# Last two expert blocks formed from PSUM in two extra output tiles of a one-core hybrid decoder step

## The reference, cut to what matters

```python
def hier_moe(h, ...):                       # 1056 tokens: 1024 prompt rows and 32 sample rows
    ...                                     # group, then two experts of 32 per token, with gates
    order = jnp.argsort(e_flat)             # the 2112 assignments sorted by expert
    padded = (counts + MOE_BLOCK - 1) // MOE_BLOCK * MOE_BLOCK
    ...
    def expert_block(args):                 # 128 rows of one expert
        e, tok = args
        xb = x_pad[tok]
        hmid = jax.nn.silu(xb @ w_gate[e]) * (xb @ w_up[e])
        return hmid @ w_down[e]
    out = lax.map(expert_block, ...) * buf_w[:, None]
    y = jax.ops.segment_sum(out, buf_tok, num_segments=n_tok + 1)[:n_tok]
...
h = x + mix                                 # decoder_layer
h = h + hier_moe(rms_norm(h, norm_ffn_w), ...)
y_prompt, y_sample = rms_norm(yp, norm_final_w), rms_norm(ys, norm_final_w)
```

## Time and profile before

| what | value |
|---|---|
| time, median of 3 runs (lowest to highest) | 1505.89 us (1504.56 to 1506.14) |
| time of the profiled execution | 1505.11 us |
| its span in the trace | 1503.4 us |
| busy PE / DVE / ACT / POOL | 1416.1 / 1061.5 / 766.1 / 568.4 us |
| HBM read / written | 316.52 MB / 59.64 MB |

### The profile page before, as it was taken

The page is one execution under the profiler, slowest core; times in us unless marked ns, Lnnn a source line. Parts: engine busy times, 40 slices in busy tenths (PEclk is TensorE's granted clock), DMA queues, the critical chain, the costliest instruction groups (busy, mean ns, idle before and its releaser), DMA issues. The chain is left out here.

```text
span 1503.4 us, 21686 instructions
## 1 busy us (share of the span) xinstructions
PE 1416.1 (94%) x7625; PEld 1233.0 (82%) x7625; DVE 1061.5 (71%) x1225; ACT 766.1 (51%) x891; POOL 568.4 (38%) x345
## 2 busy tenths in 40 slices
PE   6999999999999999899999659999999999999976
PEld 5999999999999998788877548888888888888852
DVE  6687722366666664545463579999999999999956
ACT  6332222333333335344433438777777777777734
POOL 2323324454444442485644014333433333333311
PEclk9999999999999999999999669999999999999997
DMA  5222333234444445876653659999999999999958
GB/s 197 65 78 86 126 95 111 80 130 143 144 141 147 138 144 167 294 219 239 209 168 130 231 201 383 402 396 390 377 381 362 389 379 383 385 388 387 369 211 343
DMA packets 115793, 361.07 MB, mean 240 GB/s; under 512 B 18772, under 2 KB 48468, under 8 KB 99348
## 3 DMA queue, kind: packets, MB, share of 16 engines
q1 hardware_dynamic: 100164, 322.37, 58.6%
q0 software_dynamic: 15568, 37.87, 7.3%
HBM read 316.52 MB, written 59.64 MB: 250 GB/s over the span
## 5 line engine op out<-in xcount | busy, mean ns | idle before, releaser
L2048 DVE TENSOR_TENSOR wgu_l<-wgu,wgu_h 128x2048 fp32r<-128x2048 f32 x128 | 290.0, 2288 | 27.4 <-ACT wgu_h L1928 26.5
L1928 ACT CAST wgu_h<-wgu 128x2048 fp32r<-128x2048 f32 x124 | 237.4, 1915 | 100.6 <-PE bank0and L64 100.5
L62 PE MATMUL bank0and<-wgu_h,xh_blk 128*128 128x512 f32 x512 | 203.7, 398 | 2.9 <-DVE xl_blk L2052 2.9
L64 PE MATMUL bank0and<-wgu_h,xl_blk 128*128 128x512 f32 x512 | 200.9, 392 | 0.0
L62 PE MATMUL bank0and<-xh,wh 128*128 128x352 f32 x576 | 197.6, 343 | 3.0 <-ACT raw L906 3.0
L63 PE MATMUL bank0and<-wgu_l,xh_blk 128*128 128x512 f32 x512 | 200.3, 391 | 0.0
L64 PE MATMUL bank0and<-xh,wl 128*128 128x352 f32 x576 | 186.7, 324 | 0.0
L63 PE MATMUL bank0and<-xl,wh 128*128 128x352 f32 x576 | 186.5, 324 | 0.0
L1671 POOL TENSOR_TENSOR wol<-wo,woh 128x1024 fp32r<-128x1024 f32 x48 | 121.4, 2536 | 123.5 <-ACT woh L996 123.5
L1835 POOL DMA_INDIRECT scratch_picked<-yb,dst x31 | 92.7, 2991 | 197.5 <-DVE yb L2042 197.5
L2057 DVE TENSOR_TENSOR wd_l<-wd,wd_h 128x1024 fp32r<-128x1024 f32 x128 | 148.2, 1219 | 1.2 <-ACT wd_h L1934 1.0
(11 more groups left out here) (496 smaller groups left out, 3234.5 us busy)
## 6 DMA issues: line engine op xcount, KB each, us to landing
wgu<-in_w_gate_up SPq DMA_DIRECT2D x128, 1024.0 KB, 7.6
wd<-in_w_down SPq DMA_DIRECT2D x128, 512.0 KB, 7.6
wo<-in_w_out SPq DMA_DIRECT2D x48, 512.0 KB, 4.9
w<-in_w_in_tiles SPq DMA_DIRECT2D x36, 512.0 KB, 3.6
yy<-scratch_picked SPq DMA_DIRECT2D x8, 1024.0 KB, 12.6
scratch_xb<-stage POOLq DMA_DIRECT2D x10, 512.0 KB, 4.0
xb<-scratch_xb SPq DMA_DIRECT2D x8, 640.0 KB, 4.4
scratch_uT<-feat SPq DMA_DIRECT2D x8, 528.0 KB, 5.0
```

The lines of the kernel that those rows point to most:

```text
L62: nc.tensor.matmul(acc, lh, rh, start=start, stop=False)
L64: return nc.tensor.matmul(acc, ll, rh, start=False, stop=stop)
L1928: nc.scalar.copy(wgu_h[:, s], wgu[:, s]).then_inc(gu_high, 1)
L2048: nc.vector.tensor_tensor(wgu_l[:, s], wgu[:, s], wgu_h[:, s].bitcast(F32), ALU.subtract).then_inc(gu_split, 1)
```

## The change: what it does

There is no `combine` stage any more; its work stands at the end of `experts`, without a meeting of the engines ahead of it.

- The last two blocks are never scattered to `picked`. In their place POOL scatters zeros (`yb`, set by a memset) to their rows at the start of the expert stage, between the gather for block 1 and that for block 2.
- SP loads the norm's weight and tiles 0 to 3 of h right behind the gate and up loads of block 1, tiles 8 and 4 ahead of the last block's down loads and 5 to 7 behind them. The nine `yy` loads wait for the scatter of block 29 (`y_stored`) and for PE's last `gate_up`, and go to places that the gate and up weights leave free.
- Tiles 8, 1, 0 and 3 are added on DVE, tiles 2, 4, 5, 6, 7 on PE. PE's list has tile 2 in banks 0 and 1, 4 in 6 and 7, 5 in 2 and 3, 6 in 4 and 5, 7 in 0 and 1 again. Tile 5 waits for DVE to have read banks 2 and 3 (`add_late(0)`), tile 6 for banks 4 and 5 (`add_late(1)`).
- Tile 9 holds the tokens of the last block but one, tile 10 those of the last. For each, POOL gathers the gates from a small DRAM table (`gates`, 1056 rows of two numbers, stored by SP as its first act in the stage), the rows of h, and from `picked` the row of the token's other expert. DVE adds h, gate times the other row, and gate times the PSUM result (`add_late`). Since a token may be in both blocks, tile 9's sum is also scattered back to h, and tile 10's rows of h are gathered after that has landed.
- DVE's order: add 8, late sum of 9, add 1, norms 8 and 9, add 0, norms 1, 0, 2, add 3, norms 4, 3, 5, late sum of 10, norms 6, 10, 7.
- All outputs go to one tensor `y` through indirect DMAs of POOL. Tokens of the last two blocks get a row number out of range in their ordinary tile (`out_row`), so that only tiles 9 and 10 write them.

```diff
@@ SyncE
+            sp.dma_start(S["gates"][0:SEQ, :].rearrange("(t p) k -> p t k", p=P), S["gate"][:, 0:NT, :]).then_inc(gates_stored, 16)
...
             load_gate_up(1)
+            sp.wait_ge(rows_ready, 1)
+            sp.dma_start(w_final[:], A["norm_final_w"][0].partition_broadcast(P)).then_inc(h_loaded, 16)
+            for t in range(FIRST):
+                sp.dma_start(h[t], S["h"][t * P:t * P + P, :]).then_inc(h_loaded, 16)
...
             sp.wait_ge(y_stored, m * 16 + 32)
+            for t in (8, 1, 0, 2, 3, 4, 5, 6, 7):
+                used = 0 if t == 0 else (t + 1) // 2
+                if used:
+                    sp.wait_ge(gu_used, m * 4 + (4 + used))
+                sp.sem_inc(holder, 1)
+                sp.dma_start(yy[t][0:live(t)], picked[t * P:t * P + live(t)]).then_inc(loaded[t], 16)
@@ GpSimd
+            gather(1, 1)
+            for j in range(2):
+                if j:
+                    pool.wait_ge(y_stored, 16)
+                then_own(pool, nc.gpsimd.tensor_copy(dst[:], of_row[:, 1, bass.ds(m + (1 + j), 1)]), index_copied, j + 2)
+                pool.indirect_dma_start(out=S["picked"], ..., in_=yb[:], ...).then_inc(y_stored, 16)
+            gather(2, 4)
...
+            for j in range(2):
+                late_gather(j, late_gate[:, j, :], S["gates"])
+            late_gather(0, h[NT + 1], S["h"])
+            pool.wait_ge(xT_psum, m * 2 + 6)
+            pool.wait_ge(y_stored, m * 16 + 48)
+            late_gather(0, other[0], S["picked"], 2)
+            pool.wait_ge(down_split, m * 4 + 12)
+            pool.wait_ge(xg_loaded, m * 16 + 112)
+            late_gather(1, other[1], S["picked"], 2)
+            pool.wait_ge(y_done, m + 2)
+            pool.indirect_dma_start(out=S["h"], ..., in_=total[0], ...).then_inc(y_stored, 16)
+            store(0)
+            pool.wait_ge(y_stored, m * 16 + 64)
+            late_gather(1, h[NT + 2], S["h"])
+            for n in range(1, NT + 3):
+                ...
+                store(n)
@@ TensorE
+            for n, t in enumerate(ON_PE):
+                is_loaded(pe, t)
+                if 2 <= n < 4:
+                    pe.wait_ge(y_done, m + (n - 1))
+                if n == 4:
+                    pe.wait_ge(out_ready, ORDER.index(ON_PE[0]) + 2)
...
@@ VectorE
+            def add_late(j, loads):
+                dve.wait_ge(xg_loaded, m * 16 + loads)
+                dve.wait_ge(down_used, (m + j) * 4 + 4)
+                after(nc.vector.scalar_tensor_tensor(out=h[NT + 1 + j], in0=other[j], scalar=late_gate[:, j, 1:2], in1=h[NT + 1 + j],
+                                                     op0=ALU.mult, op1=ALU.add))
+                nc.vector.scalar_tensor_tensor(out=total[j], in0=(S["banks23"], S["banks45"])[j][:], scalar=late_gate[:, j, 0:1],
+                                               in1=h[NT + 1 + j], op0=ALU.mult, op1=ALU.add).then_inc(y_done, 1)
...
-ON_PE = [1, 3, 5, 7]
-ORDER = [8, 0, 1, 2, 3, 4, 5, 6, 7]
+ON_PE = [2, 4, 5, 6, 7]
+ON_DVE = [8, 1, 0, 3]
+ORDER = [8, 9, 1, 0, 2, 4, 3, 5, 6, 10, 7]
```

More of the change, by code:

```diff
@@ new lines, in _ @@
+            gather(2, 4)
+            with pool.Fori(1, m + 1) as i:
+                gather(i + 2, i * 2 + 3)
+                scatter(i - 1, i * 2 + 4)
+            scatter(m, m * 2 + 5)
+            pool.wait_ge(rows_ready, 2)
+            then_own(pool, nc.gpsimd.memset(late_gate[:], 0.0), zeroed, 3)
+            for j in range(2):
+                for k in range(3):
+                    nc.gpsimd.tensor_copy(late_row[:, j, k:k + 1], of_row[:, k, bass.ds(m + (1 + j), 1)]).then_inc(zeroed, 1)
@@ L2039, in unload_y @@
             def unload_y(i):
-                wait(dve, y_stored, i * 16)
+                dve.wait_ge(y_stored, i * 16 + 32)
                 dve.wait_ge(down_used, i * 4 + 4)
@@ new lines, in _ @@
+            make_diag(0)
+            make_diag(1)
+            gated(m + 1)
+            low_down(m + 1, range(2))
+            low_hid(m + 1, (last_h, last_l))
+            dve.wait_ge(hT_psum, m + 2)
+            for n in range(2, len(ON_PE)):
+                make_diag(n)
+            low_down(m + 1, range(2, 4))
+            add(NT)
+            dve.wait_ge(y_stored, m * 16 + 32)
+            dve.wait_ge(xg_loaded, m * 16 + 96)
+            dve.sem_inc(holder, 1)
+            after(nc.vector.tensor_tensor(second[:], late_row[:, :, 1:2], late_row[:, :, 0:1], ALU.is_gt))
@@ new lines, in _ @@
+            after(nc.vector.tensor_tensor(step[:], late_gate[:, :, 1:2], late_gate[:, :, 0:1], ALU.subtract))
+            after(nc.vector.tensor_tensor(step[:], step[:], second[:], ALU.mult))
+            after(nc.vector.tensor_tensor(late_gate[:, :, 0:1], late_gate[:, :, 0:1], step[:], ALU.add))
+            after(nc.vector.tensor_tensor(late_gate[:, :, 1:2], late_gate[:, :, 1:2], step[:], ALU.subtract))
+            add_late(0, 96)
+            add(1)
+            norm(NT)
+            norm(9)
@@ L2221 @@
+            add(0)
+            norm(1)
+            norm(0)
+            norm(2)
+            add(3)
+            norm(4)
+            norm(3)
+            norm(5)
+            add_late(1, 128)
+            norm(6)
+            norm(10)
+            norm(7)
+FIRST = 4
+ON_PE = [2, 4, 5, 6, 7]
+ON_DVE = [8, 1, 0, 3]
+ORDER = [8, 9, 1, 0, 2, 4, 3, 5, 6, 10, 7]
 OUTPUTS = {
-    "y_prompt": (SEQ, D), "y_sample": (TS, D), "conv_tail": (P, CT_N, DEC_B + 1, CONV_K - 1),
+    "y": (T, D), "conv_tail": (P, CT_N, DEC_B + 1, CONV_K - 1),
@@ L2226 @@
     "z": (T, D), "xb": (T, D + GROUPS * NSTATE), "bct": (2 * GROUPS * NSTATE, T), "uT": (D, T), "v": (T, D), "yT": (D, T),
-    "h": (T, D), "hn": (T, D), "picked": (2 * T, D),
+    "h": (T, D), "hn": (T, D), "picked": (2 * T, D), "gates": (T, 2),
 }
```

269 lines of the change are left out of this document (137 added, 132 removed).

## The result

The changed kernel takes 1516.56 us, the median of 4 runs (1516.33 to 1518.26), against 1505.95 for the kernel before on the same chip: ratio 1.0077, 95% interval 1.0064 to 1.0089. That is slower, as forecast, but by 10.6 us and not 3.5, and it lies above the predicted range (1504 to 1515). The profiled execution took 1516.33 us with a span of 1514.3, 10.9 more than before.

The account below looks back on a forecast made before the run. Bound: the end by the yy loads, those by the last scatter. Late sum of tile 10 at 1484.5, plus 16.15 and 5.6 gives 1506.3; plus 0.6 start, span 1506.9; as median 1509.4 us, range 1504 to 1515.

Parts of the forecast that it names:

- the span ends 1.2 us later: End of the kernel: 1.2 us from the last store's landing to the span's end, within 5.6 us after DVE's end.
- What held up the loads before: Kernel before: SP issues the yy loads only at 1464.55, since the last scatter must land and the stages meet.
- The end of the loads: yy loads, moved 19.5 us earlier with the same 20.8 us, end near 1467, or near 1470 beside gathers and stores.
- The wait ahead of the late sum of tile 9: DVE waits 1.0 us (0 to 4) there for the row of the other expert, landing about 1457.4.
- The start: Expert stage's start: zero scatters ahead of block 2's gather cost 0.6 us (0 to 6); SP's early loads nothing.
- ScalarE's waits: DVE reaches norms 0, 2, 3 and 5 before ACT has their roots: 1.6 us of waits.
- The bank wait: PE's tile 6 waits for the late sum of tile 10; 16.15 us from there to DVE's end, 1500.7.
- The last store: Now indirect on POOL: 0.85 us to start, 1.0 to do, 2.55 to land after its end.
- Rival A: PE's tile 6: banks don't hold PE back, DVE's last norms follow without a wait; 1497.1 us, chance 0.12.
- Rival C: POOL at about 901 us: block 2's gather late, PE loses 4 to 6 us; 1513.8; 0.23 with tile 10's late chain.
- B: Rival of no measurable change: PE's clock recovers, the other row lands in time, the start is free; 1506.2 us, chance 0.25.

Follow-up runs that it names:

- e5: Changed kernel with one added GpSimd drain, after the store of tile 5 and ahead of that of tile 6: 1509.25 us, ratio to before 1.0028.
- e9: e1 with one added GpSimd drain in its idle time ahead of the scatter of block 29: 1502.98 us, ratio to before 0.9979.
- e6: Changed kernel with a semaphore of its own for the load of tile 8, not shared with tile 1: 1515.65 us, ratio to before 1.0065.
- e13: Kernel before with the norm weight and four tiles of h loaded ahead of the loop over the blocks: 1504.65 us, ratio 0.9992.
- e1: Changed kernel with tiles 6 and 7 summed in banks 0/1 and 6/7: 1507.27 us, ratio to before 1.0008.
- e7: Changed kernel with the memset of yb behind the gather of block 1, not at the stage's start: 1516.52 us, one run.
- e10: e9 plus SP waiting for final landings, yb memset behind block 1's gather, norm weight and four h tiles loaded behind the loop: 1499.56 us, ratio to before 0.9960.
- e2: Kernel before with its nine final stores indirect instead of direct: 1505.93 us, ratio 0.9998.
- e3: Changed kernel with SP, not GpSimd, waiting for the final stores to land: 1513.59 us, ratio to before 1.0048.
- e12: Kernel before with one more GpSimd memset (yb) at the start of the expert stage: 1505.78 us, ratio 1.0006.

## Why the prediction was wrong

- **The step that failed: "the span ends 1.2 us later"** than the last landing. The term came from the kernel before and was taken for a constant. It is 0.4 us and GpSimd's drain, which grows with its transfers (0.78 us for 9, 6.76 for 82), and by merging the two stages the change leaves all 82 to the very end. The sum had 5.6 us from VectorE's end to that of the span; measured are 1514.3 - 1503.12 = 11.2. e5 and e9 show it by moving the drain.
- **What held up the loads before** was put down to the last scatter. It had landed by 1461.3; from there to 1464.3 it was the same drain, in the meeting. The change takes these 3.0 us away and pays 6.0 more at the end.
- **The end of the loads** was summed wrongly: the 20.8 us count from 1469.61, the last issue, so 19.5 us earlier is 1470.9 and not 1467. The last load was issued at 1457.6 and landed at 1480.4. Nothing waited for the last ones, so this cost nothing.
- **The wait ahead of the late sum of tile 9** was put down to the other expert's row, 1.0 us. That row was there in time; the add of tile 8 waited 2.53 us, since its semaphore counts tile 1's load too: tile 8's own load has landed at 1449.55 + 5.2 = 1454.75, before VectorE is ready. Its loads began at 1449.55 and not 1445, because block 29's scatter landed after 8.4 us. The wait was found in the wrong place, 1.5 us too short; e6 shows that its true price is less, for other waits take its place.
- **The start** was priced at 0.6 us, for a late gather. Measured: VectorE is ready 0.75 us later than that. The memset, which I had not priced, holds up one step by 0.7 us; about 1 us at the end of the stage goes with memset, loads and zero scatters together, for a reason that stays open. That the loads alone cost nothing was right (e13).
- **ScalarE's waits,** 1.6 us, were 0.15 + 0.47 + 0.46 = 1.1 up to that point. VectorE's work between 1455.25 and 1487.10, less all waits, is 28.0 us, as summed.
- **The bank wait** was right in place and size: 16.02 us from the late sum to VectorE's end, against 16.15. That was in part luck: the idle time ahead of it was 5.9 us and not 12, since TensorE had begun tile 2 only at 1463.5, and the granted clock was 0.50 (1.2 GHz) all the same.
- **The last store:** 0.79 + 0.96 + 2.24 us against 0.85 + 1.0 + 2.55.
- **Rival A** did not happen, and e1 shows what it is worth: 8.4 us. **Rival C** did not either: the gather of block 2 started at 902.65, ahead of VectorE's splits, and TensorE waited 0.8 us for it, where it had waited 0.6. **B** was too low, by the same closing term.
- The rule of the Trainium skill (SBUF — State Buffer, its section on the two separate sides) on the shared port pair says also that a GpSimd instruction, once begun, holds the pair against some VectorE ones. The memset ends at 865.07 and the 0.86 us step at 865.10: the trace agrees. I had weighed the rule at the stores, where it costs little (0.96 us beside an idle VectorE, at most 1.60 beside its adds), and not at the memset, where it held up the step by 0.7 us. What the prediction takes from this page of the Trainium skill stands there in the section on who interferes with whom, not in the one on the DMA port swizzle.

## What to carry to other kernels

When two stages are merged, ask what the meeting between them used to do on each engine, not only what it made wait; GpSimd's drain over 64 transfers stood there, half of it beside the landing of the last scatter. Read the empty end of a span as work that has a cause and look for sequencer instructions in it, and put a drain into an idle time of GpSimd if many of its transfers come before. A bank that is read last is the wrong one for the next sum, and where two loads share a count, the first user waits for both. Taking away one of several waits in a chain (e6, e7) may give nothing. e10, with the bank and drain edits in place, gains 3.4 us over e9; how much each of its three further edits gives isn't separated.

## What the runs showed of the hardware

- A drain of GpSimd in this kernel's last stages costs 0.08 us for each transfer that it has issued since it last drained (82: 6.76 us, 63: 5.21, 19: 1.60, 9: 0.78, 3: 0.29), with nine direct ones as with nine indirect ones (e2: 0.78). It runs beside a landing if GpSimd doesn't wait for that itself (e3: 2.4 us less between last store and end), and the profile shows the engine as idle meanwhile.
- A GpSimd memset of 128x1024 stretches a VectorE step of 128x32 from 0.18 to 0.86 us (e12: 0.87).
- After 5.86 us without a matmul TensorE's granted clock was 0.50 (1.2 GHz), and the half tile took 4.9 us, not 2.6.
